# A seventh place for expert weights in a routed-expert step: x1 lent out, saved and brought back

## What is computed

```python
h = rmsnorm(x) ;  b_a, c_a, v_a, v_b, g_b = split(h @ w_in)
z = concat(b_a * dwconv3(c_a * v_a), silu(layernorm(dwconv31(v_b * sigmoid(g_b)) + bias)))
x1 = x + z @ w_out
t = rmsnorm(x1)
grp = argmax(t @ w_coarse) ; two best of the 8 experts of that group, with weights p1, p2
x2 = x1 + sum_i p_i * (silu(t @ w_gate[e_i]) * (t @ w_up[e_i])) @ w_down[e_i]     # 32 experts in all
y = rmsnorm(x2)
```

## Time and profile before

| | |
|---|---|
| median of 3 runs | 536.22 us (533.67 to 538.4) |
| the profiled execution | 534.13 us, of which its span (first to last instruction) is 532.3 us |
| PE busy in the span | 479.5 us (90%) |
| DVE, ACT, POOL busy | 239.6, 100.5, 203.8 us |
| moved by DMA | 141.25 MB, mean 265 GB/s |
| stage of the blocks | from about 270 us to about 504 us of the span |

### The profile page before, as it was taken

How to read it: one execution, slowest core, us unless ns; L and a number is a source line. 1 busy time by engine, 2 the same in 40 slices (tenths; PEclk the granted TensorE clock), 3 DMA queues, 4 the chain that set the end, 5 groups by cost and what they waited for, 6 DMA issues and landing times.

```text
span 532.3 us, 8869 instructions
## 1 busy us (share of the span) xinstructions
PE 479.5 (90%) x3269; PEld 281.5 (53%) x3270; DVE 239.6 (45%) x514; ACT 100.5 (19%) x204; POOL 203.8 (38%) x282
## 2 busy tenths in 40 slices
PE   6999999999999999999689988998998793998883
PEld 4777777777777445554344444443444341444431
DVE  3309999999987322345722221222211210221246
ACT  3331000111104432324301011111011100011214
POOL 3013929929598400111243334434344322244100
PEclk9999999999999999999699999999999987999998
DMA  8995008000000796033969899999999999999477
GB/s 335 323 392 134 0 1 316 0 2 0 1 1 1 243 422 262 39 103 133 407 239 411 296 417 421 400 398 418 418 418 420 418 420 420 418 418 421 192 275 260
DMA packets 34565, 141.25 MB, mean 265 GB/s; under 512 B 10160, under 2 KB 10176, under 8 KB 22249
## 3 DMA queue, kind: packets, MB, share of 16 engines
q1 hardware_dynamic: 28250, 127.91, 61.1%
q0 software_dynamic: 4960, 9.45, 4.8%
q10 hardware_dynamic: 1327, 3.49, 1.8%
HBM read 134.47 MB, written 13.17 MB: 277 GB/s over the span
## 4 chain that ended last, share of the span: by engine, by line
PE 68%; DMA 14%; DVE 5%; issue 5%; SPq 4%; ACT 2%; POOL 1%; DVEq 0%; POOLq 0%; ACTq 0%
PE bank L1284 25%; PE bank L1370 10%; PE bank L1488 7%; PE bank L1483 7%; PE bank L1508 7%; DMA z<-in_w_up 6%; DMA region_x<-in_w_up 6%; PE bank L1291 4%; SPq L411 2%; DMA slot<-y_rows 2%; PE bank L1436 1%; PE bank L1396 1%; PE bank L1248 1%; PE bank L1498 1%; DVE ua L1179 1%
## 5 line engine op out<-in xcount | busy, mean ns | idle before, releaser
L1284 PE MATMUL bank<-region_h,region_w 128*128 128x256 f32 (+1 forms) x544 | 132.7, 406 | 0.0
L1284 PEld LDWEIGHTS bank<-region_h,region_w 128*128 128x128 f32 x544 | 103.2, 190 | 28.2
L1177 DVE TENSOR_TENSOR ua<-ua,bank 128x128 f32<-128x128 f32 x30 | 8.6, 288 | 172.4 <-ACT ua L647 172.4
L1370 PE MATMUL bank<-region_w,z 128*128 128x512 f32 x128 | 56.7, 596 | 0.2 <-ACT z L592 0.2
L1508 PE MATMUL bank<-region_w,ua 128*32 128x512 f32 x328 | 49.9, 598 | 3.3 <-DVE ua L1179 3.3
L731 POOL TENSOR_TENSOR ub<-region_x 128x512 f32<-128x512 f32 x4 | 31.4, 7843 | 53.0 <-ACT region_x L535 53.0
L936 DVE SCALAR_TENSOR_TENSOR z<-ub,par,z 128x512 f32<-128x512 f32 x60 | 48.5, 808 | 0.0
L800 POOL COPY gcol<-gidx 128x1 uint32 (+1 forms) x30 | 5.4, 180 | 107.2 <-DVE sb_rows L1166 107.2
L936 DVE SCALAR_TENSOR_TENSOR region_x<-ub,par,region_x 128x512 f32<-128x512 f32 x56 | 45.2, 808 | 0.0
L1488 PE MATMUL bank<-region_w,z 128*32 128x256 f32 x512 | 43.5, 396 | 0.0
L1370 PEld LDWEIGHTS bank<-region_w,z 128*128 128x128 f32 x128 | 23.8, 190 | 28.0 <-issue 26.3
(11 more groups left out here) (244 smaller groups left out, 680.5 us busy)
## 6 DMA issues: line engine op xcount, KB each, us to landing
region_w<-in_w_down SPq DMA_DIRECT2D x21, 1024.0 KB, 15.5
region_w<-in_w_gate SPq DMA_DIRECT2D x16, 1024.0 KB, 13.3
region_w<-in_w_up SPq DMA_DIRECT2D x16, 1024.0 KB, 15.4
region_w<-in_w_in SPq DMA_DIRECT2D x3, 2048.0 KB, 21.3
slot<-in_w_gate SPq DMA_DIRECT2D x6, 1024.0 KB, 14.6
slot<-in_w_up SPq DMA_DIRECT2D x6, 1024.0 KB, 14.8
slot<-in_w_down SPq DMA_DIRECT2D x6, 1024.0 KB, 14.1
region_x<-in_w_up SPq DMA_DIRECT2D x5, 1024.0 KB, 23.5
```

The source lines that it names most:

```text
L1284: ins = mm(ps[2 * bank + j][:, 0:LEN[j]], sec[name][:, k, c * P:(c + 1) * P], hT[:, k, CUT[j]], start=(k == 0), stop=(k == KC - 1))
L1370: ins = mm(ps[2 * (t % 2) + j][0:n, :], z[:, k, t * P:t * P + n], w_out_sb[:, k, j * 512:(j + 1) * 512], start=(k == order[0]), stop=(k == ...
```

## The change

There is a seventh place, `EXTRA = 6`, in `region_h`, where x1 is: gate and up over the columns of x1's tiles 0 to 3, and the first half of down over tile 4; the second half of down lies in an unused stretch of `ub`. It holds position 6 and no other. The order of SP's queue becomes: after the early loads the second half of down of position 6; then x1's tiles 0 to 2 are written to a new scratch tensor `x1_rows` as they come; gate of position 6 when tiles 0 and 1 are free; position 3 as before; x1's tiles 3 and 4; position 4 after `x1_free(NT)`, which besides `s_h2` waits for the transposes and for all five writes of x1 to have landed; gate of 5 as before; up and the first half of down of position 6. Position n from 7 to 12 goes to place n - 7, whose last expert was position n - 7. From 13 on a position goes to place (n - 1) mod 6, whose last expert was position n - 6. Behind the last weights SP reads x1 back, five transfers, and DVE and PE wait for them (`s_x1b`) ahead of the first use of x1 at the end. PE's code has four pairs written out and then a loop of four turns with three pairs each, with none after it. The pair that `turns` moves to the end is picked from pair 4 on, not from pair 3 on.

```diff
+        extra_gu = RH[:, 0:2 * PART]
+        extra_dn = [RH[:, 2 * PART:2 * PART + D], ub_t[:, 0:D]]
...
+            sp.dma_start(extra_dn[1], down[:, EXTRA, 1, :]).then_inc(s_wextra[2], 16)
...
+            def save_x1(t):
+                sp.wait_ge(s_x1, 2 * t + 2)
+                sp.dma_start(x1_rows(t), x1[0:TROWS[t], t, :]).then_inc(s_x1d[min(t // 2, 1)], 16)
+
+            def x1_free(n):
+
+                sp.wait_ge(s_h2, n)
+                sp.wait_ge(s_x1t, 2 * n)
+                sp.wait_ge(s_x1d[0], 16 * 2)
+                if n > 2:
+                    sp.wait_ge(s_x1d[1], 16 * (n - 2))
+
+            def load_extra(part):
+                sp.dma_start(extra_gu[:, part * PART:(part + 1) * PART], parts[part][:, EXTRA, :])\
+                  .then_inc(s_wextra[part], 16)
+
+            for t in range(3):
+                save_x1(t)
+            x1_free(2)
+            load_extra(0)
             sp.wait_ge(s_o, NT)
             load_expert(3, 3)
-
-            sp.wait_ge(s_h2, NT)
-            load_part(4, 0, 4)
-            load_part(4, 1, 4)
-            load_part(4, 2, 4)
+            for t in range(3, NT):
+                save_x1(t)
+            x1_free(NT)
+            for part in range(3):
+                load_part(4, part, 4)
...
             load_part(5, 0, 5)
+            load_extra(1)
+            sp.dma_start(extra_dn[0], down[:, EXTRA, 0, :]).then_inc(s_wextra[2], 16)
             sp.wait_ge(s_tab, 1)
...
+            def turn(n, back):
+
+                return number(n + ORDER, 0, NE - 1), number(n + (1 - back), 1, NBLK)
...
-            with sp.Fori(1, NE // NSLOT) as it:
-                for i in range(NSLOT):
-                    reload(i, *turn(it, i), range(3))
+            for n in range(NSLOT + 1, FIXED + NSLOT):
+                reload((n - 1) % NSLOT, *turn(n, NSLOT + 1 if n < 2 * NSLOT + 1 else NSLOT), range(3))
+            with sp.Fori(2, (NE - FIXED) // NSLOT) as it:
+                for j in range(NSLOT):
+                    reload((j + 1) % NSLOT, *turn(it * NSLOT + (j + FIXED - NSLOT), NSLOT), range(3))
...
+            for t in range(NT):
+                sp.dma_start(x1[0:TROWS[t], t, :], x1_rows(t)).then_inc(s_x1b, 16)
...
-                link(nc.vector.tensor_reduce(least, key[:, NSLOT // 2:NPAIR], AX.X, ALU.min))
+                link(nc.vector.tensor_reduce(least, key[:, FIXED // 2:NPAIR], AX.X, ALU.min))
...
             dve.wait_ge(s_gfin, 16)
+            dve.wait_ge(s_x1b, 16 * NT)
...
-            for m, (after, last) in enumerate(round0):
-                pair(0, 2 * m, end, after, last)
+            for places, turns, (after, last) in zip(((0, 1), (2, 3), (4, 5), (EXTRA, 0)),
+                                                    ((0, 0), (0, 0), (0, 0), (0, 1)), ahead):
+                pair(places, turns, end, after, last)
                 end = last
-            with pe.Fori(1, NE // NSLOT) as it:
+            with pe.Fori(1, (NE - FIXED) // NSLOT + 1) as it:
                 end = None
-                for i in range(0, NSLOT, 2):
-                    end = pair_of(it, i, end)
-            for i in range(0, NE % NSLOT, 2):
-                pair_of(NE // NSLOT, i)
+                for m, (places, more) in enumerate((((1, 2), 0), ((3, 4), 0), ((5, 0), 1))):
+                    end = pair_of(it * (NSLOT // 2) + (m + (FIXED - NSLOT) // 2), places, (it, it + more), end)
...
             pe.wait_ge(s_diag, 2 * len(BY_PE))
+            pe.wait_ge(s_x1b, 16 * NT)
```

More of the change, by code:

```diff
@@ L270, in build_step @@
         s_wexp = [[sem(f"s_wexp{i}_{n}") for n in ("gate", "up", "down")] for i in range(NSLOT)]
+        s_wextra = [sem(f"s_wextra_{n}") for n in ("gate", "up", "down")]
+        s_x1d = [sem(f"s_x1d{i}") for i in range(2)]
+        s_x1b = sem("s_x1b")
         s_yg = [[sem(f"s_yg{k}_{t}") for t in range(NT)] for k in range(2)]
@@ L406, in _ @@
                      a["w_down"][0].rearrange("e (p c) d -> p e (c d)", c=F // P))
+            down = a["w_down"][0].rearrange("e (p c) d -> p e c d", c=F // P)
             def load_part(i, part, e):
@@ L1462, in _ @@
             ins.then_inc(s_inv, 1)
-            wgu = [w.rearrange("p (w k f h) -> p w k h f", w=2, k=KC, h=2) for w in slot_gu]
-            wdn = [w.rearrange("p (c d) -> p c d", c=F // P) for w in slot_dn]
+            wgu = [w.rearrange("p (w k f h) -> p w k h f", w=2, k=KC, h=2) for w in slot_gu + [extra_gu]]
+            wdn = [[w[:, c * D:(c + 1) * D] for c in range(F // P)] for w in slot_dn] + [extra_dn]
             H = T // 2
@@ L1475, in tokens, with matrices, block_of @@
                 return ins
-            def block_of(g, halves, turn):
+            def matrices(i, turn):
+                for part in range(2):
+                    if i == EXTRA:
+                        pe.wait_ge(s_wextra[part], 16)
+                    else:
+                        pe.wait_ge(s_wexp[i][part], turn * 16 + 16)
+            def block_of(g, halves, turns):
                 pe.wait_ge(s_xt, g + 1)
@@ L1502, in block_of @@
                 pe.wait_ge(s_yc, g + 1)
-                for i in sorted(set(halves)):
-                    pe.wait_ge(s_wexp[i][2], turn * 16 + 16)
+                for i, turn in dict(zip(halves, turns)).items():
+                    if i == EXTRA:
+                        pe.wait_ge(s_wextra[2], 32)
+                    else:
+                        pe.wait_ge(s_wexp[i][2], turn * 16 + 16)
                 for c in range(F // P):
@@ L1516, in bounds, with pair, pair_of @@
                 return pe.snap(both >> BITS), pe.snap(both & ((1 << BITS) - 1))
-            def pair(it, i, first, after, end):
-                for part in range(2):
-                    pe.wait_ge(s_wexp[i][part], it * 16 + 16)
+            def pair(places, turns, first, after, end):
+                i, j = places
+                matrices(i, turns[0])
                 with pe.If(after > first + 1):
                     with pe.Fori(first, after - 1) as g:
-                        block_of(g, (i, i), it)
-                for part in range(2):
-                    pe.wait_ge(s_wexp[i + 1][part], it * 16 + 16)
-                block_of(after - 1, (i, i + 1), it)
+                        block_of(g, (i, i), (turns[0], turns[0]))
+                matrices(j, turns[1])
+                block_of(after - 1, (i, j), turns)
                 with pe.If(end > after):
                     with pe.Fori(after, end) as g:
-                        block_of(g, (i + 1, i + 1), it)
-            def pair_of(it, i, first=None):
+                        block_of(g, (j, j), (turns[1], turns[1]))
+            def pair_of(m, places, turns, first=None):
                 if first is None:
-                    first = pe.value_load(bound[0:1, bass.ds(it * NSLOT + i, 1)], min_val=0, max_val=NBLK - 1)
-                after, end = bounds(bound[0:1, bass.ds(it * (NSLOT // 2) + (i // 2 + ENDS), 1)])
-                pair(it, i, first, after, end)
+                    first = pe.value_load(bound[0:1, bass.ds(m * 2, 1)], min_val=0, max_val=NBLK - 1)
+                after, end = bounds(bound[0:1, bass.ds(m + ENDS, 1)])
+                pair(places, turns, first, after, end)
                 return end
@@ L1540, in _ @@
             pe.wait_ge(s_tab, 1)
-            round0 = [bounds(bound[0:1, ENDS + m:ENDS + m + 1]) for m in range(NSLOT // 2)]
+            ahead = [bounds(bound[0:1, ENDS + m:ENDS + m + 1]) for m in range(FIXED // 2)]
             pe.wait_ge(s_mv, 1)
```

20 lines of the change are left out of this document (13 added, 7 removed).

## The result

| | before | after |
|---|---|---|
| median of 13 runs | 537.81 us (533.09 to 540.13) | 539.86 us (536.81 to 543.22) |
| the profiled execution | 534.13 us | 541.03 us |
| its span | 532.3 us | 539.3 us |

The ratio is 1.008, with a 95% interval from 1.0053 to 1.0106. On a kernel of 537 us that is 4.3 us slower (2.8 to 5.7), inside the range of the forecast, and within 1%. The two medians of the table are only 2.05 us apart; measured once more, at the end of the experiments, the change has a ratio of 1.0066 and medians 4.6 us apart. So the slowdown is clear, and its size is known to a microsecond or two. The two profiled executions are 6.9 us apart. What follows explains those two; the ratio says that about 4.3 us of it is typical.

The account below looks back on a forecast made before the run. The prediction took the weight stream from position 13 on to be clocked by block 10's gate and up, not bandwidth all the way. Terms -0.6 + 2.3 - 0.5 - 0.8 = +0.4 us gave 536.6 us, range 531.6 to 542.5.

Parts of the forecast that it names:

- rival B: Weight stream is the limit all the way, so the end comes a position sooner: -7.5 us, 528.7 us; chance 0.10.
- term 5: Position 6's loads and x1's saves go behind early loads or into the idle 210 to 234 us: no cost.
- term 1: Queue ahead of position 13: the residue of up to 1.3 us is gone; -0.6 us, bounds -1.3 and 0.
- term 3's exit: Edge out of PE's loop, block 28 to 30, goes away: -0.8 us, bounds -0.8 and 0.
- term 2: First gather, ahead of block 1, meets a position 4 delayed by x1's saves: +2.3 us, between 0 and 2.9.
- term 4: PE's granted clock may fall at block 1 after a pause: 0 in the sum, 1.6 us held for the range.
- Rival C: Slower: late first gather, clock low for two blocks, and a stall in the written-out pair; +7.1 us, 543.3 us; chance 0.10.
- term 3's entry: Edge into PE's loop, before block 8, moves behind block 10: -0.5 us, bounds -1.04 and +1.0.
- term 6: x1 read back behind the last weights lands at 505 to 506 us, worst case 509: 0, bound +1.
- A: The forecast itself: nothing comes of the seventh place, 536.6 us, own bounds -3.1 to +6.5 us; chance 0.80.

Follow-up runs that it names:

- the mended kernel: The changed kernel with x1's tiles 3 and 4 saved behind the first gather and PE's end filler ahead of the wait for x1: 534.56 us, ratio 0.9954 to the kernel before.

## Why the prediction was right and wrong

**Right: what bounds the stream.** The core of the forecast was that SP's queue runs dry before position 13, though its share reads 1.00, and that position 13 hangs on block 10. Issued 0.14 us after that block's silu, after 16.4 us of wait, and landed in 5.3 us: this is the row the prediction asked for. Taking the earlier issue away changed nothing that the runs can tell (1.0088 against 1.008), so rival B is refuted by test. The pause is 337 to 345 us instead of the 332 to 340 that I named, since block 10 came 5.7 us later.

**Right: term 5.** The idle stretch took the loads at no cost.

**Right in its sign, too small: term 1.** Forecast -0.6, bound -1.3; the profiles with and without the earlier issue say about -1.5 from block 10 to block 30, and position 13 lands in 4.8 to 5.3 us instead of 6.1 to 6.9.

**Right by luck: term 3's exit.** Between blocks 28 and 30 the edge out of the loop took 0.7 us with it (forecast 0.8). But the edge into the loop, now behind block 10, puts 1.0 there (7.99 us from block 10 to 11, 7.01 before), which the prediction left out because it "no longer matters to position 13". The layout alone is worth nothing from block 10 to block 30. What the sum has for that stretch, -1.4 for terms 1 and 3 together, is what was found, -1.3, by two errors that cancel.

**Right in its result, mis-sized on the way: term 2.** The first gather waited 2.2 us longer, as forecast (+2.3), but the delay of position 4 behind it was mis-sized. I had position 4 over 4.3 us later, from bytes and one fixed part. It was issued 7.1 us later (263.11 against 255.98), after SP had waited 11.1 us for the saves to land. What the sum left out is position 3: its 3.15 MB, 7.4 us at 424 GB/s, are issued from 249.25 to 250.6, right ahead of the two saves. In the kernel before, position 4 is issued while position 3 is still on its way; now it waits until position 3 is through, then the saves, and then their fixed part, in which the DMA engines stand idle (a share of 0.10 from 262 to 264 us). So a full position stood in the queue with the gather, and not the end of one. The Trainium skill, "DMA: Bandwidth & Descriptors", "Queues, rings and completion order", says that a DMA engine takes turns between its queues packet by packet. The measured waits agree with a gather that shares and does not pass: 3.4 to 4.6 us in the kernels with little in the queue, 6.4 to 7.8 in those with the saves or position 4 there.

**Wrong: term 4, at zero.** I left the clock out of the sum and called 1.6 us a block its price. It fell: 272 to 278 us at 0.51, and from tokens to silu block 1 took 8.17 us instead of 5.43, +2.7. The row for it was in my hands: block 22, 2.05 us of pause and 1.6 lost. I had weighed it against block 28, whose pause cost nothing, and taken the kinder one. A term that a late gather makes likely has to be in the sum with it. How long the pause is hung on one more thing: the 24 filler matmuls ahead of block 1 run at 1.2 GHz until the granted clock rises (0.50 in the rows from 260 to 264 us), and took from 5.4 to 8.3 us in the profiles. Where they took over 8, a gather as late as this one left PE idle for 0.7 or 0.9 us and the clock stayed up. Rival C had this term in full; its price of 2.9 + 3.2 at block 1 is near to the 5.35 us found there. It was the gather with the clock, and not the written-out pair, that made most of it.

**Not borne out: term 3's entry.** Forecast -0.5. The written-out pairs had a pause of 1.7 us by "issue" at block 6 (+2.1 on its interval), -0.6 at block 7 and -1.2 at block 8: +0.3 in all. In the other profiles with at least four pairs written out, the same stretch, block 5 to block 8, is from 0.9 us shorter to 1.4 longer than before, so that one profile can't tell. As a part of the whole this came out at nothing: the layout alone has 0.9993.

**Wrong: term 6, by its logic.** x1 was there at 512.40, 3.4 us past my worst case of 509, in a run whose blocks were 4.3 us late; that alone would have been small. The error was to ask only when PE wants x1. I wrote that PE "has then only the read-back of y to wait for". But 3.70 us of x1 matmuls and 7.07 us of filler stand on PE's queue between x1 and the first use of y, and before the change all of it fitted with 0.76 us to spare. With the pause, the clock went down here too, and the 3.70 became 6.41. The slack of the instruction that comes last was what to read, and it was 0.76 us, not the 1 to 2 us for which PE might wait. The ledger has 2.3 us for it. The runs with the end mended give 1.0 to 1.7 us, at the edge of noise, and their profile shows that most of what is gained at the first combination can be lost again to a later y.

The sum was +0.4 against +4.3 measured, which is nearer to C's +7.1 than to the forecast; C was worth more than its 0.10. The outcome stays within 1% because the largest claim held, and the three misses all have the same sign. In the profile they are 4.9 us at block 1 instead of 2.3, 0.3 instead of -0.5 at the loop's entry, and 2.7 instead of 0 from block 30 to the end. Two of them are beyond their own bounds, block 1 (2.9 and 1.6 for the clock) and the end (+1), and the profile's +7.0 is beyond A's +6.5; that the runs lie inside is in part luck. A smaller flaw is that 536.6 stood on a median of three runs, 536.22, and with 13 it was 537.81. What stays open is the pause at block 6, which the same layout in the kernel before shows too (an interval of 8.4 us), what sets the time of y's last tile, and about 1 us of the mended kernel's gain.

## What to carry to other kernels

A buffer more brings a stream forward only as far as it is used: one used once moves the first waits and leaves the next one where it was, and the row to look for is the first reload whose condition does not change. Count what stands in the queue when a small, urgent transfer comes, and move bulk writes behind it; two writes, 0.79 MB together, moved with their wait behind one issue were worth 1% here. When a load is put in front of a wait, ask for the slack of the last instruction behind it, with all that stands between, and keep in the sum that a pause of TensorE may be paid twice, the second time in clock.

## What the runs showed of the hardware that was not expected

- **Code is fetched through the DMA engines, and a loop can be too long.** A PE loop of three pairs caused no fetches while it was repeated; loops of six and seven pairs were fetched again in their second turn, in packets of 16 KB: 37 and 36 in all, where 20 and, for ten pairs written down with a short loop, 25 were enough. With the DMA engines full of weights this gave pauses of up to 10.6 us by "issue" and cost 1.25% with no other change. The idle time in this form does not name its cause; the instruction queue's packets do.
- **A small gather in a full queue takes about twice its time**: 3.4 to 4.6 us against 6.4 to 7.8 over the kernel before and those derived from it; which of the two it was went with whether the saves of x1, or a position 4 issued just before it, were in the queue.
- **Short pauses may or may not take the clock down.** PE's idle of 0.7 and 0.9 us ahead of the first block left it up, those of 2.2 to 3.5 us ahead of it were each followed by a fall, which in the change took 2.7 us from the block behind it. A wait of 2.05 us ahead of block 22 was followed by one too, and one of about the same length ahead of block 28 was not.
- **A save that is waited for costs more than its bytes.** SP waited 11.1 us for two writes of x1, 0.79 MB, which are 1.9 us at 424 GB/s. They stood behind 3.15 MB of weights in the same queue (7.4 us), and near the end of the wait the DMA engines moved almost nothing (a share of 0.10 for 2 us).
